# Inputs laid out for the chip, modulation products as one VectorE operation each, and a first pair of units worked off by k tiles

## What is computed

```python
h = concatenate([meta, x], axis=1)                       # 16 + 256 tokens
xn = rms_norm(h, norm_g)                                 # first norm
q, k, v, f_logit, o_gate = split(xn @ w_in, ...)         # fox_in, and 16 forget logits
...
mod = (silu(c) @ w_ada + b_ada).reshape(b, 3, 3, D)      # 9216 numbers
def sublayer(h, i, fn, resid_w):
    shift, scale, gate = mod[:, i, 0], mod[:, i, 1], mod[:, i, 2]
    u = rms_norm(h, norm_pre[i]) * (1 + scale) + shift
    return h + resid_w * gate * rms_norm(fn(u), norm_post[i])
```

## Time and profile before

| | |
|---|---|
| median of three runs | 1377.29 us (1376.18 to 1378.13) |
| the profiled execution, its own time | 1374.68 us |
| its span in the profile | 1373.0 us |
| TensorE (PE) busy | 1326.5 us, 97% |
| VectorE (DVE) busy | 988.0 us, 72% |
| ScalarE (ACT) busy | 626.4 us, 46% |
| data moved | 252.20 MB, mean 184 GB/s |

### The profile page before, as it was taken

The page is one execution under the profiler, slowest core; times in us unless marked ns, Lnnn a source line. Parts: engine busy times, 40 slices in busy tenths (PEclk is TensorE's granted clock), DMA queues, the critical chain, the costliest instruction groups (busy, mean ns, idle before and its releaser), DMA issues.

```text
span 1373.0 us, 28199 instructions
## 1 busy us (share of the span) xinstructions
PE 1326.5 (97%) x11291; PEld 1277.5 (93%) x11291; DVE 988.0 (72%) x1362; ACT 626.4 (46%) x722; POOL 72.1 (5%) x103
## 2 busy tenths in 40 slices
PE   7999999999999899999999999999999999999998
PEld 6998799999999888999999999999998899999986
DVE  6666788887677764888866787777877457986644
ACT  5266553444354244544443533433544664544433
POOL 4000000000001000000000011101011000000000
PEclk9999999999999999999999999999999999999999
DMA  7752265657865333555677588997476334575543
GB/s 212 214 153 63 76 223 162 197 174 199 231 194 179 116 94 123 185 184 184 196 206 220 181 268 273 274 254 241 150 234 215 118 129 158 192 232 180 186 155 123
DMA packets 243806, 252.20 MB, mean 184 GB/s; under 512 B 4809, under 2 KB 228300, under 8 KB 243732
## 3 DMA queue, kind: packets, MB, share of 16 engines
q1 hardware_dynamic: 232464, 211.96, 50.5%
q0 software_dynamic: 11072, 39.14, 8.5%
q10 hardware_dynamic: 196, 0.06, 0.0%
HBM read 250.08 MB, written 1.05 MB: 183 GB/s over the span
## 4 chain that ended last, share of the span: by engine, by line
PE 73%; DVE 12%; ACT 8%; issue 5%; DMA 1%; DVEq 0%; ACTq 0%; SPq 0%
PE ps L2233 59%; ACT w_hi L466 5%; PE ps L2855 4%; DVE w_lo L1112 4%; PE ps L2256 2%; DVE proj L1132 1%; PE ps L2447 1%; DMA raw<-in_ffn_w_down 1%; PE ps L2199 1%; PE ps L2382 1%; PE ps L2620 1%; ACT scratch L684 0%; DVE x_lo L1300 0%; PE ps L2497 0%; DVE proj L1598 0%
## 5 line engine op out<-in xcount | busy, mean ns | idle before, releaser
L1112 DVE TENSOR_TENSOR w_lo<-raw,w_hi 128x2048 fp32r<-128x2048 f32 (+1 forms) x185 | 443.1, 2395 | 206.5 <-ACT w_hi L466 205.4
L2233 PE MATMUL ps<-x_hi,w_hi 128*128 128x258 f32 (+2 forms) x2016 | 581.6, 288 | 5.6 <-DVE w_lo L1112 2.3
L2233 PE MATMUL ps<-x_hi,w_lo 128*128 128x258 f32 (+2 forms) x2016 | 574.4, 285 | 1.7 <-issue 1.7
L466 ACT ACTIVATE w_hi<-raw 128x2048 fp32r<-128x2048 f32 (+1 forms) x185 | 369.4, 1997 | 388.2 <-PE ps L2233 337.6
L2233 PE MATMUL ps<-x_lo,w_hi 128*128 128x272 f32 (+2 forms) x1856 | 528.9, 285 | 0.0
L2233 PEld LDWEIGHTS ps<-x_hi,w_hi 128*128 128x128 f32 x2016 | 382.3, 190 | 9.6 <-issue 3.9
L2233 PEld LDWEIGHTS ps<-x_hi,w_lo 128*128 128x128 f32 x2016 | 382.5, 190 | 2.0 <-issue 2.0
L2233 PEld LDWEIGHTS ps<-x_lo,w_hi 128*128 128x128 f32 x1856 | 351.8, 190 | 0.3
L2233 PE MATMUL ps<-g_hi,w_hi 128*128 128x256 f32 (+1 forms) x576 | 164.2, 285 | 4.9 <-DVE w_lo L1112 2.4
L2233 PE MATMUL ps<-g_hi,w_lo 128*128 128x256 f32 (+1 forms) x576 | 162.8, 283 | 0.0
L2233 PE MATMUL ps<-g_lo,w_hi 128*128 128x256 f32 (+1 forms) x576 | 162.2, 282 | 0.0
(11 more groups left out here) (382 smaller groups left out, 1601.1 us busy)
## 6 DMA issues: line engine op xcount, KB each, us to landing
raw<-in_ffn_w_gate SPq DMA_DIRECT2D x44, 1024.0 KB, 5.4
raw<-in_ffn_w_up SPq DMA_DIRECT2D x44, 1024.0 KB, 5.4
v_tok<-in_w_ada POOLq DMA_DIRECT2D x72, 512.0 KB, 4.7
raw<-in_ffn_w_down SPq DMA_DIRECT2D x24, 1408.0 KB, 7.1
raw<-in_w_in SPq DMA_DIRECT2D x20, 1024.0 KB, 5.2
raw<-in_hgrn_w_in SPq DMA_DIRECT2D x16, 1024.0 KB, 5.6
raw<-in_fox_w_in SPq DMA_DIRECT2D x15, 1024.0 KB, 5.9
raw<-in_ffn_w_down SPq DMA_DIRECT2D x11, 1024.0 KB, 4.9
```

Source lines behind the costliest of these rows:

```text
L466: nc.scalar.activation(w_hi[s][:, 0:size], raw[s][:, 0:size], ACT.Copy).then_inc(hi_ready, 1)
L1112: V.tensor_tensor(w_lo[s][:, 0:size], raw[s][:, 0:size], w_hi[s][:, 0:size].bitcast(F32), ALU.subtract).then_inc(lo_ready, 1)
L2233: ins = T_.matmul(dst, fixed, moving, start=(kt == 0 and i == 0), stop=(kt == kts - 1 and i == 2))
```

## The change

1. **Inputs.** The host now hands over the 272 tokens turned and tiled (`h_t`, [128, 8, 272]), all gain and bias vectors as columns (`vec_cols`), the forget weights (`w_f`), the lambda rows in one piece and w_ada by output column (`w_ada_t`, [128, 72, 1024]: partition m of tile t holds the 1024 inputs of output column 128 t + m). All transposes at the start go, and most of the small transfers.
2. **w_ada.** Each half step is now one load of [128 x 1024] (4 KB in a row for each partition) and one `scalar_tensor_tensor` with `accum_out`, which multiplies by silu(c) spread over all partitions (`c_row`) and sums along the free axis straight into a column of `mod`. `ada_sums`, its waits and the semaphore chain of VectorE go. `ada_half` now stands ahead of `split_lo`. For `c_row`, TensorE makes eight fp32 matmuls of 128 columns at the start, and ScalarE copies them out of PSUM in two operations.
3. **The first pair of units.** h and the first unit's weights come in four groups of two k tiles, alternating on SyncE's queue, each with its own semaphore; ScalarE and VectorE split each group's activations and weights in turn; TensorE goes through unit 0 by k tiles, as they come. Before that it makes `WARM` = 11 matmuls of ones. Unit 1 comes in two halves.
4. **Forget logits** are now 24 fp32r matmuls in three passes (x_hi, x_lo with `w_f_hi`, `w_f_lo`, split by GpSimd), without the transposes behind them. The loads of the later vectors (`more_landed`) are issued after unit 1's weights have landed.
5. **Waits.** `head_sums` on TensorE no longer waits for `vec_ready` (VectorE's copies of the turned vectors), but for `c_row_set`. ScalarE waits for the second step's products before it writes into `v_tok` in the attention.

```diff
+WARM = 11
...
             def ada_half(p, s):
...
-                for k in range(KD // 2):
-                    c_k = c_silu[:, KD // 2 * s + k:KD // 2 * s + k + 1]
-                    if s == 0 and k == 0:
-                        ins = V.tensor_scalar(ada_acc, ada_raw[s][:, k, :], c_k, None, ALU.mult)
...
+                V.scalar_tensor_tensor(out=v_tok[:, s, :], in0=v_tok[:, s, :], scalar=1.0, in1=c_row[:], op0=ALU.mult, op1=ALU.mult,
+                                       accum_out=total).then_inc(ada_mult, 1)
...
+                            if ada and not early:
+                                ada_half(it + (first - ada_it), s2)
                             if size and not (ahead and s2 == 0) and not (defer and s2 == 1):
                                 split_lo(pair + 1, s2, size)
-                            if ada and not early:
-                                ada_half(it + (first - ada_it), s2)
...
+            for g in range(4):
+                kts = slice(2 * g, 2 * g + 2)
+                sp.dma_start(h[:, kts, :], dram["h_t"][:, kts, :]).then_inc(x_landed[g], 16)
...
+                sp.dma_start(first_w[:, kts, :], fox_w[:, kts, 0:UNIT_W]).then_inc(raw_landed[0] if g == 3 else w_landed[g], 16)
...
+            for g in range(4):
+                first_tiles_hi(g)
+                first_weights_hi(g)
+            for n, bank in enumerate((5, 7)):
+                act.wait_ge(c_spread, n + 1)
+                nc.scalar.activation(c_row[:, n * 512:(n + 1) * 512], ps[:, bank, :], ACT.Copy).then_inc(c_row_set, 1)
...
-            def ada_sums(p):
-
-                pe.wait_ge(ada_mult, p * 2 + 4)
-                for s in range(2):
-                    T_.matmul(ps[:, 5, bass.ds(p * 2 + (ADA_COL + s), 1)], ada_sum[:, s * P:(s + 1) * P], ones[:, 0:1],
-                              start=True, stop=True).then_inc(ada_done, 1)
...
+            pe.wait_ge(warm_set, 1)
+            for _ in range(WARM):
+                T_.matmul(ps[:, 6, 0:P], rstd[:, 0:P], rstd[:, 0:P], start=True, stop=True)
+            pe.wait_ge(ident_landed, 16)
+            pe.wait_ge(c_ready, 1)
+            for n, bank in enumerate((5, 7)):
+                for i in range(4):
+                    k = 4 * n + i
+                    ins = T_.matmul(ps[:, bank, i * P:(i + 1) * P], c_silu[:, k:k + 1].to_broadcast([P, P]), ident, start=True, stop=True)
+                ins.then_inc(c_spread, 1)
...
+                for kt in range(KD):
+                    if kt % 2 == 0:
+                        pe.wait_ge(x_lo_ready, kt // 2 + 1)
+                        if kt == KD - 2:
+                            pe.wait_ge(lo_ready, 3)
+                        else:
+                            pe.wait_ge(part_lo, kt // 2 + 1)
+                    tile_products(kt, 0)
...
+                for k in range(KD):
+                    for i, (wt, x) in enumerate(((w_f_hi, x_hi), (w_f_hi, x_lo), (w_f_lo, x_hi))):
+                        ins = T_.matmul(ps[0:F_ROWS, 6, 0:L], wt[:, k, :], x[:, k, :], start=(k == 0 and i == 0), stop=(k == KD - 1 and i == 2))
...
-                pe.wait_ge(vec_ready, 4)
+                pe.wait_ge(c_row_set, 2)
```

More of the change, by code:

```diff
@@ L1354, in _ @@
-            V.tensor_tensor(w_lo[0][:, UNIT // 2:UNIT], raw[0][:, UNIT // 2:UNIT], w_hi[0][:, UNIT // 2:UNIT].bitcast(F32), ALU.subtract).then_inc(lo_ready, 1)
-            for g in range(1, 4):
-                first_tiles_out(g)
-            split_lo(0, 1, UNIT)
-            sum_squares(0, L)
-            dve.wait_ge(vec_turned, 1)
-            V.tensor_copy(cols[:, 0, 0:VEC_ROWS[0]], ps[:, VEC_AT[0][0], 0:VEC_ROWS[0]]).then_inc(vec_ready, 1)
-            dve.wait_ge(vec_ready, 1)
+            dve.wait_ge(c_gate, 1)
@@ L1362, in _ @@
+            dve.wait_ge(cols_landed, 16)
+            steps.done(V.tensor_scalar(c_silu, c_silu, 1.0, None, ALU.add))
+            steps.wait()
+            steps.done(V.reciprocal(c_silu, c_silu))
+            steps.wait()
+            V.tensor_tensor(c_silu, c_silu, vecs("c_2", 0, KD), ALU.mult).then_inc(c_ready, 1)
             for i in range(2):
@@ L2216, in unit_pair @@
                             lo = w_lo[s][:, 0:g["size"]].rearrange("p (k m) -> p k m", m=width)
-                            if halves and first and s == 0:
-                                pe.wait_ge(half_lo, 1)
-                            else:
-                                pe.wait_ge(lo_ready, pair * 2 + (s + 3))
+                            pe.wait_ge(lo_ready, pair * 2 + (s + 3))
                             pe.wait_ge(banks_free[s], pair + 1)
@@ L2287, in gemm @@
                     start += int(peel)
[L2288 to L2289 removed]
+                    turns = sorted({start, end, *(n for a in by_tokens for n in (a, a + 1))})
                     for a, b in zip(turns, turns[1:]):
                         if a in by_tokens:
[L2292 removed]
+                            unit_pair(a, swap=True)
                             continue
                         with pe.Fori(a, b) as it:
[L2295 removed]
+                            unit_pair(it)
             def from_tiles(m, n):
@@ L2383, in head_sums @@
                 ins.then_inc(hq_ss, 1)
-            gemm("fox_in", from_first, xh, xl, L, k=0, late=first_norm_sum, after=forget_logits, ada="fox_in", sums=(2, 4), halves=True)
+            first_pair()
+            forget_logits()
+            gemm("fox_in", from_norm(0), xh, xl, L, k=0, its=(1, 4))
             gemm("fox_in", from_norm(0), xh, xl, L, k=1, after=head_sums)
```

388 lines of the change are left out of this document (165 added, 223 removed).

## The result

The changed kernel takes 1354.22 us (median of four runs, 1350.98 to 1356.99), against 1377.28 for the kernel before: a ratio of 0.983, 95% interval 0.981 to 0.985. The forecast was 1350.9, in a range of 1344 to 1362. Five more runs of the changed kernel on another chip gave 1350.62 (1347.73 to 1353.14); the median of all nine is 1353.1. So 23 us came off where the sum had 26.4; the forecast's own 26.4 was made against the profiled execution (1374.7), and between the two profiled executions it is 20.8.

The account below looks back on a forecast made before the run. TensorE, busy for 97% of the span, was taken to bound the kernel. 13.5 + 4.4 + 1.2 + 8.3 - 1.0 = 26.4 us off the profiled 1374.7 gives 1348.3, or 1350.9 for the median; range 1344 to 1362.

Parts of the forecast that it names:

- Part 1: Modulation sums (ada_sums) taken from TensorE: 33 of 36 steps at 0.41 us, 13.5 us gained (12 to 16).
- Part 2: VectorE's modulation as two 1.3 us operations a step, hidden under w_hi; freed waits for w_lo gain 4.4 us (1.5 to 5.5).
- The loss in fox_out: First w_ada load after the attention holds up split_lo on VectorE: 1.0 us lost (0 to 2).
- Part 3: TensorE's wait before the first head_sums, set by vec_ready, goes: 1.2 us gained.
- Part 4: The start: unit 2's first product at 24.5 us instead of 32.85, 8.3 us gained; best case 9.5.
- Half rate: Rival: VectorE's accumulating operation streams at half rate, 2.35 us a half step; some 6 us less gain, 1357; chance 0.12.
- The weight loop: Rival: weight loads of 6.2 us or more beside w_ada set the pace instead of TensorE; 13.5 us less, 1364; chance 0.08.
- Late w_ada: Rival: VectorE waits for w_ada before each split; beyond about 10.6 us, each microsecond costs 36; slower, 1401 at 12; chance 0.03.

Follow-up runs that it names:

- e5: Changed kernel with the forget weights' split waiting for its own load alone and the later small loads issued after the third unit's weights; 1349.60 us, ratio 0.981.
- e3b: Changed kernel with w_ada loads cut to a 32nd of the bytes from the third step on, same operations; 1345.53 us, ratio 0.977.
- e7: Kernel before with w_ada loads cut to a 32nd of the bytes from the third step on; 1375.14 us, ratio 0.999.
- e4b: Kernel before without TensorE's matmuls for the modulation sums; 1367.26 us, ratio 0.993.
- e1: Changed kernel with split_lo put back ahead of the modulation half step in VectorE's order; 1353.91 us, ratio 0.983.
- e2: Changed kernel with w_ada laid out tile by tile, so each load reads one contiguous block; 1352.70 us, ratio 0.983.
- e8: Kernel before with both small w_ada loads and no TensorE matmuls for the modulation sums; 1363.78 us, ratio 0.990.

## Why the forecast was right, and what it missed

- **TensorE sets the end.** Right: 97% before and after.
- **Part 1, 13.5 us.** The mechanism was right, and the price of 0.37 to 0.45 a step is exact where the loop is in step. The count was too high: alone it gave 9.8 us. I excluded three steps that end in a wait; there were more, in ffn1_down, ffn0_up, hgrn_in and at the start of glu1_down, and I had counted those same waits in part 2.
- **Part 2.** The operation takes 1.228 us for 1.29 forecast. The waits of ffn1_down are gone. The 0.98 at the end of glu1_down, half of which I counted, only moved to the next stage. Parts 2 and 3 less the loss were to be 4.6; what is left of 23.4 us (1376.5, the median of all runs of before, less 1353.1) after 9.8 for the sums and 7.2 for the start is 6.4. Parts 1 and 2 are better read as one: with VectorE's chain gone, the sums' time in front of those waits is gained after all.
- **The loss in fox_out, 1.0 us.** It is 1.1: 0.49 at once and the rest through the next weight load.
- **Part 3.** The 1.22 us wait is gone.
- **Part 4, 8.3 us.** It gave 7.2. I had unit 1's `w_lo` wait at 1.1 us (there was none), and took GpSimd's later loads as harmless. The logits waited 1.52 us for GpSimd's split, and these loads share the bandwidth with the third unit's load, which lands at 20.7 after 8.9 us (7.7 without them, in e5), a load that the sum did not contain.
- **Half rate.** Wrong in this case. The Trainium skill ("Vector Engine (DVE) Microarchitecture Reference", Points that are easy to get wrong) says that the form "with two non-bf16 SBUF sources halves throughput"; here it streams 1024 elements in 1228 ns with the accumulator, no slower than the plain form of the earlier trace rows, and 83 ns for reading the accumulator stand beside it.
- **The weight loop.** I gave it 0.08 and a threshold of 6.2 us (the terms as I listed them add up to 10.4, not 10.6, which makes it 6.4); the loads of glu1_up took 6.1 and 6.8. It does not take the pace of every pair, since only some loads are that long, but it is the step that was mis-sized: the traffic of w_ada, costed at nothing, costs 7.6 us by the medians of e3b, of which 2.2 to 3.3 are seen in the profiles. Without it the change is worth 29.6 us by the medians (e7 to e3b), and 26.4, the sum's own number, by their two profiles with the clock drops taken out (one execution each). My argument against it, that pairs without modulation run at 11.5 "with the same loads", left out that those pairs had no w_ada beside them.
- **Late w_ada.** VectorE waited 4.4 us in all for w_ada, at most 2.2 at once. Far from 36 x 0.73.
- **The total.** It is nearer than its terms, and that is in part luck. Part 1 was too high by 3.7 and parts 2 and 3 too low by 1.8, which partly cancel because they meet in the same waits. The start was too high by 1.1. What the traffic took is inside these numbers; the sum had nothing for it.

What stays open: why the clock drops at 436 and 528 us in some executions and not in others. The rows show that TensorE had stood still in between ahead of each drop, and that executions of one kernel differ there; no run isolates it. Whether e3b's better clock comes of its shorter waits or of chance, its five runs don't prove. And why the weight loads of the changed kernel take longer than e4b's, at the same pace and with the same bytes beside them: e1 and e2 rule out the order alone and the layout alone, and the two together were not put back.

## What to carry to other kernels

A saving per loop iteration counts only where the iteration does not end in a wait; list the waits first, iteration by iteration, and price savings that meet in one wait together. When the bounding engine gets a few per cent faster, look at what its loads have left: here the same 1 MB of traffic beside each pair went from 0.7 us to 7.6 in the whole kernel as a pair fell from 11.8 us to 11.4, and the faster pair alone (e4b against e8) accounts for about 3.5 of it. And before a difference of 2 us is believed, run the same kernel twice: two profiles of one kernel differed here by 6.2 us.

## What the runs showed of the hardware

- `scalar_tensor_tensor` on two fp32 operands in SBUF with `accum_out`: 1228 ns for 128 x 1024, and 83 ns for the read of the accumulator.
- Without `WARM` TensorE's level rose behind the second product of unit 0, and the small fp32 matmuls ahead took 3.76 us instead of 1.95.
- A short drop of TensorE to its lower level came behind waits, in some executions of a kernel and not in others, and cost 1.7 us, or 3.4 where it was twice as long. The mean clock goes with about half of the variance between executions, 1.1 us per 0.001.
- GpSimd's cast and subtraction of 128 x 384 took 0.50 and 0.99 us in the changed kernel, with VectorE idle, and 0.89 and 1.37 in e5, where VectorE was at work beside them; VectorE's three operations there took 3.13 us in all, against 2.25 in the changed kernel.
- 1 MB weight loads took 5.3 us with a 32nd of w_ada's bytes beside them (e3b), and 6.1 to 6.8 or 5.6 to 6.2 with all of them (the changed kernel's two profiles, 276 and 281 GB/s in all).
